# Second mixer: scores of two head pairs on both row halves, wider products, and the stick-breaking's sums as products of a high and a low part

## The reference

```
u, vv, q, k, v = split(rms_norm(h) @ w_in_odd)          # each 256 x 512
# gating unit, in 2 blocks of 128 positions, 4 groups of 128 channels
yc = gelu(u) * (tril(w_s) @ rms_norm(gelu(vv)) + b_s)
# stick-breaking attention, 8 heads of 64; before(t) is the positions s < t
z        = q @ k.T / 8
log_rest = where(before, log_sigmoid(-z), 0)
tail     = reversed cumulative sum of log_rest, without its own term
a        = where(before, exp(log_sigmoid(z) + tail), 0)
yd       = a @ v
h        = h + concat(yc, yd) @ w_out_odd
```

## Time and profile before

| | us |
|---|---|
| median of three runs | 620.69 |
| the three runs | 620.97, 618.47, 620.69 |
| the execution that was profiled | 618.18 |
| its span | 616.5 |

### The profile page before, as it was taken

How to read it: one execution, slowest core, us unless ns; L and a number is a source line. 1 busy time by engine, 2 the same in 40 slices (tenths; PEclk the granted TensorE clock), 3 DMA queues, 4 the chain that set the end, 5 groups by cost and what they waited for, 6 DMA issues and landing times.

```text
span 616.5 us, 8036 instructions
## 1 busy us (share of the span) xinstructions
PE 550.0 (89%) x3350; PEld 306.2 (50%) x3350; DVE 180.4 (29%) x314; ACT 176.6 (29%) x310; POOL 6.5 (1%) x16
## 2 busy tenths in 40 slices
PE   6999899999999969676799999999999999786776
PEld 4888687534443424221388877775344344141311
DVE  4787845301110101010465375353111011010101
ACT  5745635111111101010474878351110111010101
POOL 0000000000000000000000000000000000000000
PEclk7999999999999989889999999999999999898988
DMA  8999998899999999999999925797999999999994
GB/s 315 420 423 418 423 368 365 323 423 372 424 422 420 419 424 420 419 422 416 421 421 418 402 94 207 280 407 273 425 393 403 422 422 418 422 422 422 418 420 194
DMA packets 33629, 236.36 MB, mean 383 GB/s; under 512 B 3760, under 2 KB 3760, under 8 KB 5552
## 3 DMA queue, kind: packets, MB, share of 16 engines
q1 hardware_dynamic: 32800, 232.07, 92.0%
q0 software_dynamic: 784, 3.68, 1.5%
HBM read 234.68 MB, written 1.05 MB: 382 GB/s over the span
## 4 chain that ended last, share of the span: by engine, by line
PE 65%; DMA 28%; DVE 4%; ACT 2%; issue 1%; SPq 1%; DVEq 0%; ACTq 0%
DMA raw<-stream 27%; PE psum L1243 19%; PE psum L253 8%; PE psum L254 8%; PE psum L255 8%; PE psum L1220 6%; PE psum L1291 6%; DMA xT<-x_turned 1%; PE psum L1305 1%; PE psum L510 1%; PE psum L327 1%; PE psum L794 1%; ACT hidT L1364 1%; PE psum L1070 1%; PE psum L1278 1%
## 5 line engine op out<-in xcount | busy, mean ns | idle before, releaser
L1243 PE MATMUL psum<-raw,x 128*32 128x512 f32 x944 | 126.0, 639 | 35.0 <-DMA raw<-stream 25.7
L245 DVE TENSOR_TENSOR raw_lo<-raw,whi 128x1024 fp32r<-128x1024 f32 x52 | 62.4, 1222 | 45.2 <-ACT whi L238 45.1
L1243 PEld LDWEIGHTS psum<-raw,x 128*32 128x32 f32 x944 | 24.9, 111 | 99.3 <-issue 58.1
L1220 PEld LDWEIGHTS psum<-pick,h 128*128 128x128 f32 x512 | 63.2, 204 | 21.7 <-issue 18.4
L238 ACT CAST whi<-raw 128x1024 fp32r<-128x1024 f32 x52 | 53.3, 1047 | 52.3 <-PE psum L255 46.9
L1291 PE MATMUL psum<-y,pickT 128*128 128x512 f32 x128 | 63.7, 619 | 5.1 <-ACT y L1370 3.5
L1220 PE MATMUL psum<-pick,h 128*128 128x128 f32 x512 | 67.4, 291 | 0.6 <-DVE pick L1187 0.5
L1243 PE MATMUL psum<-raw,hidT 128*32 128x512 f32 x480 | 61.0, 623 | 6.5 <-ACT hidT L1364 6.5
L253 PE MATMUL psum<-whi,hnT_hi 128*128 128x512 f32 x144 | 58.1, 403 | 4.8 <-DVE hnT_lo L357 4.7
L254 PE MATMUL psum<-whi,hnT_lo 128*128 128x512 f32 x144 | 57.8, 401 | 0.0
L255 PE MATMUL psum<-raw_lo,hnT_hi 128*128 128x512 f32 x144 | 57.4, 398 | 0.0
(11 more groups left out here) (206 smaller groups left out, 485.8 us busy)
## 6 DMA issues: line engine op xcount, KB each, us to landing
raw<-stream SPq DMA_DIRECT2D x203, 1024.0 KB, 24.1
late<-stream SPq DMA_DIRECT2D x14, 1024.0 KB, 9.1
raw<-stream SPq DMA_DIRECT2D x2, 512.0 KB, 6.5
xT<-x_turned SPq DMA_DIRECT2D x2, 512.0 KB, 7.6
h<-x SPq DMA_DIRECT2D x1, 1024.0 KB, 12.0
pb<-even_bias POOLq DMA_DIRECT2D x1, 1024.0 KB, 13.8
pool_c<-even_pool POOLq DMA_DIRECT2D x1, 1024.0 KB, 10.9
pb<-even_bias POOLq DMA_DIRECT2D x1, 512.0 KB, 8.2
```

The lines of the kernel that those rows point to most:

```text
L245: nc.vector.tensor_tensor(raw_lo[ring_no(c) % RAW][:, cols], chunk(c)[:, cols], whi[:, n % SPLIT, cols].bitcast(F32), ALU.subtract).then_i ...
L1220: mm = nc.tensor.matmul(psum[:, gather_banks(q)[part], kk * P:(kk + 1) * P], h[:, t, k * P:(k + 1) * P], pick[:, t, :], start=(t == 0), st ...
L1243: nc.tensor.matmul(psum[rows, b, :], lhs[:, rows], chunk(c)[:, e * W4:(e + 1) * W4], start=start, stop=stop).then_inc(moe_used, 1)
```

## The change

- A call of `z_pe` is now for two pairs of heads (`group`), heads 0 to 3 or 4 to 7, and takes the two row halves in turn. The scores lie in four banks, 768 columns in two banks for each half.
- `sum_pe` works on two float32r copies, a high part that ScalarE casts (`stick_hi_act`) and a low part that VectorE subtracts (`stick_lo_dve`): for each, four products of 256 columns and two of 512. The mask is four products of 256 columns.
- `gating_pe` makes four products of 256 columns, each for both blocks of positions, and stands ahead of `sum_pe(pe, 0)` in TensorE's order. VectorE's eight operations behind it are four.
- `av_pe` waits for both groups' weights, since the scores now reach into bank 7; the first part of output step 1 stands ahead of it.
- The rows of the output weights are laid out on the host in the reference's order.

```diff
-        def out_step(pe, c0, order, i, hi, lo):
+        def out_step(pe, c0, order, i, hi, lo, parts=(0, 1)):
...
-            for part in range(2):
+            for part in parts:
...
-        stick = [at("stick0", [P, HALF], 36), at("stick1", [P, HALF], 42)]
+        stick = [at("stick0", [P, 2, HALF // 2], 36), at("stick1", [P, 2, HALF // 2], 42)]
+
+        stick_hi = [at("stick_hi0", [P, 2, HALF // 2], 42, F32R), at("stick_hi1", [P, 2, HALF // 2], 0, F32R)]
+        stick_lo = [at("stick_lo0", [P, 2, HALF // 2], 36, F32R), at("stick_lo1", [P, 2, HALF // 2], 42, F32R)]
...
+        ones = at("ones", [P, P], 51.5, F32R)
...
+            pe.wait_ge(od.vn_ready, T)
+            for g in range(4):
+                mm = nc.tensor.matmul(psum[:, 2 + g // 2, g % 2 * S:(g % 2 + 1) * S].rearrange("p (n t) -> p n t", n=T),
+                                      sgu[:, g * P:(g + 1) * P], vv_in[:, :, g * P:(g + 1) * P], start=True, stop=True,
+                                      skip_group_check=True)
+                if g % 2:
+                    mm.then_inc(od.gated, 1)
...
+        z_banks = psum[:, 4:8, :].rearrange("p (h b) n -> p h (b n)", h=2)[:, :, 0:HALF // 2]
...
+        def z_pe(pe, group):
             z0, z1 = half_parts(z_banks)
+            for i in range(2):
+                for par in range(2):
+                    rows = slice(64 * par, 64 * par + 64)
+                    nc.tensor.matmul(z0[:, par, i, :], kT1[rows, 2 * group + i, 0:P], qT1[rows, 2 * group + i, :],
+                                     start=(i == 0), stop=False, skip_group_check=True)
+            for i in range(2):
+                for par in range(2):
+                    rows = slice(64 * par, 64 * par + 64)
+                    mm = nc.tensor.matmul(z1[:, par, i, :], kT1[rows, 2 * group + i, P:S],
+                                          qT1[rows, 2 * group + i, P:S], start=(i == 0), stop=False,
+                                          skip_group_check=True)
+                    if i == 1:
+                        mm.then_inc(od.z_done, 1)
+        def sum_pe(pe, group):
             z0, z1 = half_parts(z_banks)
+            pe.wait_ge(od.stick_lo_ready, group + 1)
+            if group == 0:
+                pe.wait_ge(od.big_ready, 3)
+            for half in (stick_hi, stick_lo):
+                r0, r1 = half_parts(half[group][:])
+                for par in range(2):
+                    nc.tensor.matmul(z0[:, par], tri[:], r0[:, par], start=False, stop=False, skip_group_check=True)
+                    nc.tensor.matmul(z1[:, par], tri[:], r1[:, par], start=False, stop=False, skip_group_check=True)
+                    nc.tensor.matmul(z0[:, par, :, P:S], ones[:], r1[:, par], start=False, stop=False,
+                                     skip_group_check=True)
+            masks = tri[:].unsqueeze(1).to_broadcast([P, 2, P])
+            for par in range(2):
+                nc.tensor.matmul(z0[:, par, :, 0:P], bigid[:], masks, start=False, stop=True, skip_group_check=True)
+                mm = nc.tensor.matmul(z1[:, par], bigid[:], masks, start=False, stop=True, skip_group_check=True)
             mm.then_inc(od.sum_done, 1)
+        def av_pe(pe, group):
+            a0, a1 = half_parts(stick[group][:])
+            pe.wait_ge(od.stick_ready, 2)
...
             z_pe(pe, 0)
             odd_block(3)
+            gating_pe(pe)
             sum_pe(pe, 0)
-            gating_pe(pe)
             odd_block(4, (0,))
             pe.wait_ge(od.stick_ready, 1)
             z_pe(pe, 1)
-            pe.wait_ge(od.yc_ready, 8)
+            pe.wait_ge(od.yc_ready, 4)
             turn_pairs(pe, u_in, 2, od.yc_turned)
             odd_block(4, (1,))
             pe.wait_ge(od.mixC_lo_ready, 2)
             out_step(pe, OUT1, ODD_OUT, 0, mixC_hi, mixC_lo)
             sum_pe(pe, 1)
             pe.wait_ge(proj_out[1], 10)
+            out_step(pe, OUT1, ODD_OUT, 1, mixC_hi, mixC_lo, (0,))
             av_pe(pe, 0)
             av_pe(pe, 1)
-            out_step(pe, OUT1, ODD_OUT, 1, mixC_hi, mixC_lo)
+            out_step(pe, OUT1, ODD_OUT, 1, mixC_hi, mixC_lo, (1,))
             pe.wait_ge(od.mixD_lo_ready, 2)
             out_step(pe, OUT1, ODD_OUT, 2, mixD_hi, mixD_lo)
             out_step(pe, OUT1, ODD_OUT, 3, mixD_hi, mixD_lo)
...
+        def stick_hi_act(act, group):
+            act.wait_ge(od.rest_ready, 3 * (group + 1))
+            if group == 1:
+                act.wait_ge(w_used, 2 * mixer_no(OUT1))
+            nc.scalar.copy(stick_hi[group][:], stick[group][:]).then_inc(od.stick_hi_ready, 1)
+        def stick_lo_dve(dve, group):
+            dve.wait_ge(od.stick_hi_ready, group + 1)
+            nc.vector.tensor_tensor(stick_lo[group][:], stick[group][:], stick_hi[group][:].bitcast(F32), ALU.subtract
+                                    ).then_inc(od.stick_lo_ready, 1)
...
             split_hi(act, PROJ1 + 8)
+            stick_hi_act(act, 0)
             split_hi(act, PROJ1 + 9)
             block_out(act, 1, PROJ1, 3, u_in, ACT.Gelu)
             weights_act(act, 0)
...
             stick_act(act, 1)
+            stick_hi_act(act, 1)
             split_hi(act, OUT1 + 1)
...
             nc.vector.tensor_copy(tri[:], negtri).then_inc(od.big_ready, 1)
+            nc.vector.tensor_copy(ones[:], negones).then_inc(od.big_ready, 1)
...
+            stick_lo_dve(dve, 0)
             split_lo(dve, PROJ1 + 8)
...
+            for g in range(4):
+                cs = slice(g * P, (g + 1) * P)
+                dve.wait_ge(od.gated, g // 2 + 1)
+                nc.vector.scalar_tensor_tensor(u_in[:, :, cs], psum[:, 2 + g // 2, g % 2 * S:(g % 2 + 1) * S].rearrange(
+                    "p (n t) -> p n t", n=T), sgu[:, 4 * P + g:4 * P + g + 1], u_in[:, :, cs], ALU.add, ALU.mult
+                    ).then_inc(od.yc_ready, 1)
...
             stick_dve(dve, 1)
+            stick_lo_dve(dve, 1)
             split_lo(dve, OUT1 + 1)
```

More of the change, by code:

```diff
@@ L787, in hybrid_kernel @@
-        z_banks = psum[:, 4:7, :].rearrange("p b n -> p (b n)")
-        def z_pe(pe, par):
-            rows = slice(64 * par, 64 * par + 64)
-            z0, z1 = half_parts(z_banks)
[L793 to L799, removed]
@@ new lines, in av_pe @@
+        def av_pe(pe, group):
+            a0, a1 = half_parts(stick[group][:])
+            pe.wait_ge(od.stick_ready, 2)
+            for i in range(2):
+                for par in range(2):
+                    hd = 2 * (2 * group + i) + par
+                    dst = psum[64 * par:64 * par + 64, 7 - group, i * S:(i + 1) * S]
+                    nc.tensor.matmul(dst, v1_in[:, 0, hd * DH:(hd + 1) * DH], a0[:, par, i, :], start=True, stop=False,
+                                     skip_group_check=True)
+                    mm = nc.tensor.matmul(dst[:, P:S], v1_in[:, 1, hd * DH:(hd + 1) * DH], a1[:, par, i, :],
+                                          start=False, stop=True, skip_group_check=True)
+                    if i == 1:
+                        mm.then_inc(od.av_done, 1)
@@ L878, in stick_act, with stick_dve @@
             nc.scalar.activation(soft[:], soft[:], ACT.Ln, bias=1.0).then_inc(od.ln_ready, 1)
-        def stick_dve(dve, par):
-            rest = stick[par]
+        def stick_dve(dve, group):
+            rest = stick[group]
             r0, r1 = half_parts(rest[:])
-            dve.wait_ge(od.ln_ready, par + 1)
+            dve.wait_ge(od.ln_ready, group + 1)
             nc.vector.scalar_tensor_tensor(rest[:], z_banks, 0.0, rest[:], ALU.max, ALU.add).then_inc(od.rest_ready, 1)
-            dve.wait_ge(od.rest_ready, 3 * par + 1)
-            mask = before.unsqueeze(1).to_broadcast([P, 4, P])
-            nc.vector.tensor_tensor(r0[:, :, 0:P], r0[:, :, 0:P], mask, ALU.mult).then_inc(od.rest_ready, 1)
+            dve.wait_ge(od.rest_ready, 3 * group + 1)
+            mask = before.unsqueeze(1).unsqueeze(1).to_broadcast([P, 2, 2, P])
+            nc.vector.tensor_tensor(r0[:, :, :, 0:P], r0[:, :, :, 0:P], mask, ALU.mult).then_inc(od.rest_ready, 1)
@@ new lines, in stick_lo_dve, with weights_act, mixD_act @@
+        def stick_lo_dve(dve, group):
+            dve.wait_ge(od.stick_hi_ready, group + 1)
+            nc.vector.tensor_tensor(stick_lo[group][:], stick[group][:], stick_hi[group][:].bitcast(F32), ALU.subtract
+                                    ).then_inc(od.stick_lo_ready, 1)
+        def weights_act(act, group):
+            act.wait_ge(od.sum_done, group + 1)
+            nc.scalar.activation(stick[group][:], z_banks, ACT.Exp).then_inc(od.stick_ready, 1)
+        def mixD_act(act, group):
+            act.wait_ge(od.av_done, 2 * group + 2)
+            nc.scalar.copy(mixD_hi[:, 2 * group:2 * group + 2, :], bank(7 - group).rearrange("p (j s) -> p j s", j=2)
+                           ).then_inc(od.mixD_hi_ready, 1)
```

64 lines of the change are left out of this document (14 added, 50 removed).

## The result

The changed kernel takes 627.34 us (626.24 to 629.44, 4 runs), the kernel before 619.58 (617.68 to 620.97, 4 runs). The ratio is 1.0132, interval 1.0095 to 1.0169: slower by 7.8 us in the medians, where 5.8 was forecast.

The account below looks back on a forecast made before the run. TensorE was taken to carry the kernel through the second mixer, the weight stream following. Waits less savings gave 3.8 us, with 2.0 for the clock 5.8, on a base of 619.6: 625.4 us, range 620.8 to 629.5.

Parts of the forecast that it names:

- The first wait: Ahead of the second mixer's gating: TensorE idle 7.6 us for copies to `u_in`, gating from 362.35, block 4 4.1 us late.
- The clock behind it: On gating and first sums: the clock falls in the first wait and work at half rate loses 2.0 us.
- Scores: Second mixer's score products: 1.4 us a call instead of 2.81, 1.4 saved each; the first call's saving worth nothing.
- The second wait: Ahead of the second sums: TensorE waits 2.1 us while ScalarE's new cast and VectorE's subtraction make the low part.
- The second wait, 2.1 us, I count without such a loss.: At the second sums: no slow-clock loss is added behind the 2.1 us wait.
- Behind the sums: Ahead of `av_pe`: TensorE stands 0.6 us for both groups' weights; its products stay the same in number and shape.
- The sum: Whole kernel: 4.1 - 1.4 + 2.1 - 1.65 + 0.6 = 3.8 us, with the clock 5.8 slower; all behind the mixer moves equally.
- The range: Whole time: 620.8 us (clock free, 256-wide products at their low end) to 629.5 (dear products, longer slow clock, higher base).
- the clock costs nothing: Rival on the slow clock behind the wait: it adds nothing, so only +3.8 us, 623.4; chance 0.15.
- dear products: Rival on the sums: 256-wide products take 0.22 us, 0.85 more for each call, 627.1 us; chance 0.11.
- the gating does not wait: Rival at the gating: copy to `u_in` is in time, TensorE keeps its savings, 6.1 us faster, 613.5; chance 0.07.
- the delay is taken up: Rival behind the mixer: transfers go on while TensorE waits and absorb the delay; no change, 619.6 us; chance 0.07.

Follow-up runs that it names:

- e4: Changed kernel with ScalarE's copies to `u_in` ahead of the first high-part cast and the next chunk's two casts: mixer 104.6 us, median 624.36, ratio 1.0045.
- e1: Changed kernel with the gating products put back behind the first sums: mixer 104.8 us, median 623.79 us, ratio 1.0060 to the kernel before.
- e2: Changed kernel with 28 products of zeros in TensorE's wait ahead of the gating: mixer 106.0 us, median 624.57 us, ratio 1.0060 to before.
- e3: As e2, plus eight products of zeros in the wait ahead of the second sums: mixer 105.0 us, median 625.02 us, ratio 1.0073 to before.
- a1: The kernel before, unchanged, run again against itself: mixer 101.81 us, median 620.81 us, ratio 1.0011.
- a2: The kernel before, unchanged, run again for a third trace: mixer 101.80 us, median 620.62 us.
- e5: Changed kernel without high and low parts (float32 sums), gating behind the first sums: mixer 99.8 us, median 620.02 us, ratio 0.9998 to before.
- e6: Kernel before with only the gating products moved ahead of the first sums: mixer 108.8 us, median 628.02 us, ratio 1.0135.
- e7: Changed kernel's products and parts, reordered: half of block 4, first sums, then gating; casts and subtractions reordered too. Mixer 98.1 us, median 617.52, ratio 0.9965.
- e8: The order of e7 without the high and low parts, sums in float32: mixer 99.4 us, median 619.58 us, ratio 0.9981 to before.

## Why the prediction was right

It was right in the mechanism, nearly step by step, with one term missing. That the mixer's 6.35 us came so near the 5.8 is in part luck: the missing term is worth 1.5 us in the second sums, and three others that were off the other way made up for 1.2 of it. I take the mixer's start 3.21 us later in the changed kernel's trace off its rows and compare with the earlier trace rows.

- *The first wait.* The gating starts at 362.3 (362.35 forecast), wait 7.30 (7.6). e4 and e1 show both halves of the reason: ScalarE's copies are late, and the sums no longer stand in that wait.
- *The clock behind it.* Block 4 started at 368.7, 6.0 late; the forecast had 4.1 and 2.0 of clock. e2 sets its price at 2.2.
- *Scores.* 1.50 us instead of 2.81 (345.35 to 346.85, the first call), where half of the first mixer's gave 1.4. The first call's gain went into the wait, as argued.
- *The second wait.* 2.17 (2.1 forecast).
- *The step that failed: "The second wait, 2.1 us, I count without such a loss."* The clock fell behind it too, and the second sums took 3.96 us. At the full clock they take 2.47 (e3), under the 2.7 forecast, as a 256-wide product takes 0.12 us and not the 0.15 of the straight line. With zeros in the wait the mixer is 1.0 us shorter, since 0.49 of the 1.49 us goes into the wait for the exponential: that is the term that was missing. The forecast had put it at nothing without giving a reason.
- *Behind the sums.* The forecast wait of 0.6 us for the second weights did not come, since TensorE was late itself; e3, where it was not, has 0.49. The products with v took 2.80 us, not 3.11, because the 3.11 held a wait that no row calls idle. In the kernel before, the products of the second group start at 389.26, 0.48 us after the start of the first group's last row, where the same step takes 0.21 in the changed kernel. They waited for ScalarE's exponential of their weights, which ended at 389.20. That is 0.27 of the 0.31 us. In a1 and a2, too, they start 0.05 and 0.06 us behind its end. TensorE's two rows and ScalarE's one, from the kernel before:

```profile
388.78 0.44 PE L828 MATMUL psum<-stick,v_in 128*64 128x128 f32 x4
389.26 0.66 PE L826 MATMUL psum<-stick,v_in 128*64 128x256 f32 x4
...
387.75 1.45 ACT L893 ACTIVATE stick<-psum 128x1536 f32<-128x1536 f32 x1 [1.88 <-PE psum L815]
```

- *The sum.* The mixer is 6.35 us longer (5.8 forecast), the median 7.8. That all behind the mixer moves by its amount holds within the intervals for the changed kernel (1.0102 would be 6.35 us) and for all others but e5. Still, each median lies 0.4 to 2.4 us above what the mixer's length gives. In the variants of the changed kernel 0.3 to 0.4 us of that lies outside the span, which is 2.0 to 2.1 us shorter than the whole time there, and 1.7 shorter in the kernel before and in e6. The rest stays open.
- *The range.* Its lower end, 620.8, does not follow from the two terms that are named for it: 619.6 + 3.8 - 1.0 is 622.4.

Of the rivals, *the clock costs nothing* falls by e2, *dear products* by the 0.12 us, *the gating does not wait* by the 7.30 us, and *the delay is taken up* by the median and by the rest of 0.66 that the transfers still have behind the mixer. But that rest had shrunk more than the forecast said: it gave the late chunks 4 us to spare, and only about a third of 5 us was left.

Where 6.35 us come from, by mixer lengths: the scores, the wide products and the split step -2.0 (before to e5); the high and low parts, whose cast and subtraction stand in TensorE's way, +5.0 (e5 to e1); the gating ahead of the sums +3.4 (e1 to the changed kernel). The split depends on the order in which the steps are taken: in the kernel before, the same move of the gating costs 7.0 (e6). Seen the other way, the low clock behind the two waits is 3.2 of the 6.35 us (e3 against the changed kernel), the rest is the waits, less what the cheaper products save.

## What to carry to other kernels

Cheaper products pay only if the engine has something else to do while their operands are made. A call of the sums fell from 4.38 to 2.47 us on TensorE, 1.45 of it by the two one-pass parts and 0.46 by the wide mask products. The parts cost 3.2 us a call in the chain of the others: in the changed order they lost 5.0 us, in e7's order they won 1.3. When a block of work is moved, look for the wait that it used to fill, and for what an in-order engine does ahead of the one copy that ends that wait.

## What the runs showed of the hardware

- Behind an idle time of TensorE of 2.2 us in the mixer the clock fell, in all five traces that have it (the changed kernel's two, e1, e2, e4), to 1.2 GHz within 0.7 us of the wait's end. Products of zeros in the waits kept it at 2.4 GHz (e2, e3).
- Behind idle times up to 1.40 us in the mixer (e5, e7, e8), and of 1.58 us ahead of it (all 13 traces), it stayed at 2.4 GHz. But that is no safe length: among the experts of the kernel before it fell during an idle time of 1.42 us (until 537.42; 0.57 at 537 to 538 us).
- Float32r products of 256 columns start every 0.12 us, those of 128 every 0.11: below 256 columns their time is nearly the same for half as many columns. What sets it there no run tells.
- Eight float32 products with 64 rows, four of 256 columns and four of 128, take 2.81 us on one row half and 1.50 when they take the two halves in turn. They also write four banks then, not three; no run has one without the other.
